# State updates of a chunked mLSTM layer as three products of rounded halves, with one buffer for the sample states

## What is computed

```python
num = (w_inter[..., None] * jnp.einsum('bthd,bhde->bhte', qb, C)
       + jnp.einsum('bhts,bshe->bhte', S, vb))
...
C_new = w_C[..., None, None] * C + jnp.einsum('bhs,bshd,bshe->bhde', w_s, kb, vb)
n_new = w_C[..., None] * n + jnp.einsum('bhs,bshd->bhd', w_s, kb)
```

## Time and profile before

| what | us |
|---|---|
| median of 3 runs (2037.6 to 2041.7) | 2039.84 |
| the profiled execution | 2038.48 |
| its span, first to last instruction | 2036.7 |
| busy in the span: PE / DVE / ACT / POOL | 2019.5 / 1426.9 / 922.5 / 876.6 |
| chain that ended last, by engine | PE 94%, SP queue 2%, DMA, DVE, ACT and issue 1% each |

### The profile page before, as it was taken

One profiled execution on the slowest core, in us unless ns is written; L12 is line 12 of the kernel. 1 busy time (PEld: TensorE's weight loads), 2 busy tenths in 40 slices (PEclk: granted clock), 3 DMA queues, 4 the chain that ended last, 5 costly groups with the idle time before them and its releaser, 6 DMA issues.

```text
span 2036.7 us, 34175 instructions
## 1 busy us (share of the span) xinstructions
PE 2019.5 (99%) x12259; PEld 1887.3 (93%) x12259; DVE 1426.9 (70%) x2214; ACT 922.5 (45%) x1886; POOL 876.6 (43%) x721
## 2 busy tenths in 40 slices
PE   9999999999999999999999999999999999999998
PEld 5999999999999999999999999998888888888886
DVE  7667676688777676798778766664445477777775
ACT  5544445545454445445454455442224343333332
POOL 2465556575655655684555555520000123222220
PEclk9999999999999999999999999999999999999999
DMA  6643555555444565555434566568645788888765
GB/s 223 149 124 114 143 142 140 146 133 127 124 129 128 136 160 145 125 139 133 122 115 125 141 162 132 132 204 208 166 119 174 207 253 269 247 239 239 235 180 120
DMA packets 551255, 328.24 MB, mean 161 GB/s; under 512 B 283440, under 2 KB 514736, under 8 KB 551088
## 3 DMA queue, kind: packets, MB, share of 16 engines
q1 hardware_dynamic: 512960, 307.45, 56.0%
q10 hardware_dynamic: 36976, 14.42, 2.9%
q0 software_dynamic: 1152, 4.19, 0.6%
HBM read 232.42 MB, written 93.57 MB: 160 GB/s over the span
## 4 chain that ended last, share of the span: by engine, by line
PE 94%; SPq 2%; DMA 1%; DVE 1%; ACT 1%; issue 1%; POOL 0%; DVEq 0%; POOLq 0%; ACTq 0%
PE bank L712 21%; PE bank L714 21%; PE bank L713 21%; PE bank L2297 3%; PE bank L2299 2%; PE bank L2298 2%; PE bank L2267 2%; PE bank L2252 2%; PE bank L1663 1%; PE bank L1665 1%; PE bank L1664 1%; PE bank L1649 1%; PE bank L1652 1%; PE bank L1650 1%; PE bank L1614 1%; PE bank L780 1%
## 5 line engine op out<-in xcount | busy, mean ns | idle before, releaser
L712 PE MATMUL bank<-xh,wh 128*128 128x352 f32 x2688 | 869.5, 323 | 2.0 <-ACT snap L882 1.6
L714 PE MATMUL bank<-xh,wl 128*128 128x352 f32 x2688 | 866.3, 322 | 0.0
L713 PE MATMUL bank<-xl,wh 128*128 128x352 f32 x2688 | 863.0, 321 | 0.0
L1097 DVE TENSOR_TENSOR wl<-raw,wh 128x512 fp32r<-128x512 f32 x384 | 421.6, 1100 | 209.1 <-ACT wh L860 207.9
L712 PEld LDWEIGHTS bank<-xh,wh 128*128 128x128 f32 x2688 | 504.4, 188 | 5.2 <-issue 2.0
L714 PEld LDWEIGHTS bank<-xh,wl 128*128 128x128 f32 x2688 | 506.9, 189 | 0.0
L713 PEld LDWEIGHTS bank<-xl,wh 128*128 128x128 f32 x2688 | 506.0, 188 | 0.3 <-issue 0.2
L882 ACT ACTIVATE snap<-bank 128x352 f32<-128x352 f32 x384 | 178.4, 465 | 375.7 <-PE bank L714 375.6
L860 ACT ACTIVATE wh<-raw 128x512 fp32r<-128x512 f32 x384 | 240.7, 628 | 157.2 <-PE bank L714 155.7
L1097 DVE TENSOR_TENSOR wl<-wt,wh 128x512 fp32r<-128x512 f32 x288 | 235.4, 822 | 103.6 <-ACT wh L860 103.2
L660 POOL TENSOR_TENSOR stage<-snap 128x352 f32<-128x352 f32 x96 | 96.4, 1004 | 460.5 <-ACT snap L882 459.2
(11 more groups left out here) (349 smaller groups left out, 2584.4 us busy)
## 6 DMA issues: line engine op xcount, KB each, us to landing
raw<-in_w_in SPq DMA_DIRECT2D x72, 1024.0 KB, 5.7
raw<-in_w_in SPq DMA_DIRECT2D x48, 512.0 KB, 5.4
scr_vob<-stage SPq DMA_DIRECT2D x192, 88.0 KB, 3.7
scr_qk<-stage SPq DMA_DIRECT2D x48, 352.0 KB, 5.9
raw<-scr_qk SPq DMA_DIRECT2D x16, 1024.0 KB, 8.5
area<-scr_vob SPq DMA_DIRECT2D x32, 512.0 KB, 8.0
scr_acc<-x_res SPq DMA_DIRECT2D x17, 512.0 KB, 6.1
m_acc<-scr_acc SPq DMA_DIRECT2D x17, 512.0 KB, 8.0
```

The lines of the kernel that those rows point to most:

```text
L712: pe.matmul(out, wh[:, b, k, :], xh[:, b, k, :], start=(first and k == 0), stop=False, skip_group_check=True)
L713: pe.matmul(out, wh[:, b, k, :], xl[:, b, k, :], start=False, stop=False, skip_group_check=True)
L714: m = pe.matmul(out, wl[:, b, k, :], xh[:, b, k, :], start=False, stop=(k == 3), skip_group_check=True)
L1097: dve.tensor_tensor(low, source(q, b), high.bitcast(F32), ALU.subtract).then_inc(S["w_low"], 1)
```

## The change

From tile 2 on, the keys and values of the state update are split in two: ScalarE copies the weighted keys and the values with ones to rounded ones (`high`: 128x1024 each), VectorE subtracts the rounded keys from the keys (`keys_low`, in place of the keys), GpSimd the rounded values from the values (`values_low`). The update is then three products, high x high, low x high (258 columns each) and high x low (256), instead of one fp32 product. The room comes from the second buffer of the sample states: there is now one, so a unit's states are loaded once the previous unit's have been stored, and the store is issued in the unit's own tile. Arrangement and addresses besides that:

```diff
         syhl = overlay(4 * D, "m_s_y", [P, 8, 2, TS], F32R)
+        kwl0 = overlay(8 * D, "m_kwl0", [P, H, HD], F32R)
         convw = sb(ctx, "convw", [P, 2, 4, D], F32R)
...
     UNIT_LOADS = 10
-    SQUARES_FROM = 2
+    SQUARES_FROM = SPLIT_FROM = 2
     qk = qk_tiles(raw)
...
     th = [th0, wide[:, 0:1024]]
     qs = wide[:, 1024:2048].rearrange("p (f t) -> p f t", f=8)
-    kw = [a.rearrange("p (h d) -> p h d", h=H) for a in (wide[:, 2048:3072], overlay(22560, "m_kw1", [P, D])[:, :])]
+    kw = [a.rearrange("p (h d) -> p h d", h=H) for a in (wide[:, 2048:3072], overlay(22656, "m_kw1", [P, D])[:, :])]
+    kwh, kwl = overlay(0, "m_kwh", [P, H, HD], F32R), (kwl0, overlay(22656, "m_kwl1", [P, H, HD], F32R))
+    v1l, v1h = overlay(4096, "m_v1l", [P, H, HD], F32R), overlay(26752, "m_v1h", [P, H, 288], F32R)
     kb = overlay(18464, "m_kb", [P, D])
     C = wide[:, 3072:5128].rearrange("p (h d e) -> p h d e", h=H, d=2)
-    sC = (wide[:, 5128:7184].rearrange("p (b d e) -> p b d e", b=4, d=2), overlay(0, "m_s_C", [P, 4, 2, HE]))
+    sC = wide[:, 5128:7184].rearrange("p (b d e) -> p b d e", b=4, d=2)
     sq, sz, sbr = (wide[:, at:at + 128].rearrange("p (r d x) -> p r d x", r=2, d=2) for at in (7184, 7312, 7440))
...
     def states_loaded(u):
-        return S[f"states_loaded{u % 2}"], 32 * (u // 2 + 1)
+        return S["states_loaded"], 32 * (u + 1)
 
     def load_states(dma, u):
-        (i, h), p = unit(u), u % 2
+        if u >= UNITS:
+            return
+        i, h = unit(u)
+        wait(dma, S["s_stored"], 32 * u)
         for d in range(2):
             at = slice(d * P, (d + 1) * P)
-            dma.dma_start(sC[p][:, :, d, 0:HD], st_C[0, 4 * i:4 * i + 4, h, at, :].rearrange("b p e -> p b e")).then_inc(states_loaded(u)[0], 16)
+            dma.dma_start(sC[:, :, d, 0:HD], st_C[0, 4 * i:4 * i + 4, h, at, :].rearrange("b p e -> p b e")).then_inc(states_loaded(u)[0], 16)
 
...
             return
-        wait(dma, S[f"s_stored{u % 2}"], 32 * (u // 2))
         wait(dma, S["s_y_turned"], u - 1)
...
         load_keys(dma, u)
         load_rest(dma, u)
-        load_states(dma, u)
 
...
         def store_unit(u):
-            (i, h), p = unit(u), u % 2
+            i, h = unit(u)
             sp.wait_ge(S["s_C_updated"], 4 * (u + 1))
             for d in range(2):
                 at = slice(d * P, (d + 1) * P)
                 sp.dma_start(C_sample[0, 4 * i:4 * i + 4, h, at, :].rearrange("b p e -> p b e"),
-                             sC[p][:, :, d, 0:HD]).then_inc(S[f"s_stored{p}"], 16)
+                             sC[:, :, d, 0:HD]).then_inc(S["s_stored"], 16)
 
...
             residual(t)
-            if back_of(t - 1) is not None:
-                store_unit(back_of(t - 1))
             if t:
                 values(t + 2)
+                if back_of(t - 1) is not None:
+                    load_states(sp, back_of(t - 1) + 1)
                 key_squares(t + 2)
                 out_gates(t + 2)
+            if back_of(t) is not None and t < NT - 1:
+                store_unit(back_of(t))
             gates(t + 1)
...
         sp.wait_ge(S["state_stored"], 48)
-        sp.wait_ge(S["s_stored0"], 32 * 4)
-        sp.wait_ge(S["s_stored1"], 32 * 4)
+        sp.wait_ge(S["s_stored"], 32 * UNITS)
 
...
         pool.wait_ge(S["set"], 3)
+        def values_low(t):
+
+            pool.wait_ge(S["v_high"], t - SPLIT_FROM + 1)
+            pool.tensor_tensor(v1l[:, :, :], v1[t % 2][:, :, 0:HD], v1h[:, :, 0:HD].bitcast(F32), ALU.subtract).then_inc(S["v_low"], 1)
+
         for t in range(NT):
+            if t >= SPLIT_FROM:
+                values_low(t)
             ahead(t + 1)
...
                 h, d = j // 2, j % 2
-                if d == 0:
-                    pe.wait_ge(S["kw_ready"], 4 * t + h + 1)
-                m = pe.matmul(out, kw[t % 2][:, h, d * P:(d + 1) * P], v1[t % 2][:, h, :], start=True, stop=True)
+                dk = slice(d * P, (d + 1) * P)
+                if t < SPLIT_FROM:
+                    if d == 0:
+                        pe.wait_ge(S["kw_ready"], 4 * t + h + 1)
+                    m = pe.matmul(out, kw[t % 2][:, h, dk], v1[t % 2][:, h, :], start=True, stop=True)
+                else:
+                    if j == 0:
+                        pe.wait_ge(S["kw_low"], t - SPLIT_FROM + 1)
+                        pe.wait_ge(S["v_low"], t - SPLIT_FROM + 1)
+                    both = bank[DC[j % 2]][:, 0:HE + 1]
+                    pe.matmul(both, kwh[:, h, dk], v1h[:, h, 0:HE + 1], start=True, stop=False)
+                    pe.matmul(both, kwl[t % 2][:, h, dk], v1h[:, h, 0:HE + 1], start=False, stop=False)
+                    m = pe.matmul(both[:, 0:HD], kwh[:, h, dk], v1l[:, h, :], start=False, stop=True)
             else:
...
                 for j in range(4):
-                    pe.matmul(bank[SPARE][32 * j:32 * j + DT, 0:HE], sqs[:, d, DT * j:DT * (j + 1)], sC[p][:, j, d, :],
+                    pe.matmul(bank[SPARE][32 * j:32 * j + DT, 0:HE], sqs[:, d, DT * j:DT * (j + 1)], sC[:, j, d, :],
                               start=(d == 0), stop=False, skip_group_check=True)
...
 
+        def high(t):
+
+            if not SPLIT_FROM <= t < NT:
+                return
+            act.wait_ge(S["dC_summed"], updates_before(t - 1) + 8)
+            act.wait_ge(S["kw_ready"], 4 * t + 4)
+            act.activation(kwh[:, :, :], kw[t % 2], ACT.Copy).then_inc(S["kw_high"], 1)
+            act.wait_ge(S["v_ready"], 2 * t + 2)
+            act.wait_ge(S["v_padded"], 1)
+            act.activation(v1h[:, :, 0:HE], v1[t % 2], ACT.Copy).then_inc(S["v_high"], 1)
+
         def squares(t):
...
                 unit_front(front_of(t))
+            high(t + 1)
             y_high(t)
...
 
+        def keys_low(t):
+
+            if not SPLIT_FROM <= t < NT:
+                return
+            dve.wait_ge(S["kw_high"], t - SPLIT_FROM + 1)
+            dve.tensor_tensor(kwl[t % 2][:, :, :], kw[t % 2], kwh[:, :, :].bitcast(F32), ALU.subtract).then_inc(S["kw_low"], 1)
+
         def turn_o(t):
...
             for b in range(4):
-                c = sC[p][:, b, :, 0:HD]
+                c = sC[:, b, :, 0:HD]
                 dve.scalar_tensor_tensor(c, c, swcb[:, h, 4 * i + b:4 * i + b + 1],
...
         def unit_weights(u):
             dve.wait_ge(*unit_loads(u))
-            dve.tensor_copy(sC[u % 2][:, :, :, HD], n_of(u)).then_inc(S["s_n_set"], 1)
+            dve.tensor_copy(sC[:, :, :, HD], n_of(u)).then_inc(S["s_n_set"], 1)
             dve.wait_ge(S["s_kw_ready"], u + 1)
...
                     last_add(1)
+                    dve.memset(v1h[:, :, HE:HE + 1].bitcast(F32), 0.0).then_inc(S["v_padded"], 1)
             second_half(t)
...
             y_low(t)
+            keys_low(t + 1)
         dve.wait_ge(S["s_y_high"], 1)
```

More of the change, by code:

```diff
@@ L137, in layer @@
                work[:, 2104:2112], mem_k, mem_v, mv_prompt, w_out, x_prompt, x_sample, st_n)
-        recur(nc, block, X, M, overlay, bank, w, ident, raw, last_y, work, wide, syhl, area, nT, mask, smask, columns, late_w, res, yh, yl,
+        recur(nc, block, X, M, overlay, bank, w, ident, raw, last_y, work, wide, syhl, kwl0, area, nT, mask, smask, columns, late_w, res, yh, yl,
               wmh, wml, g_final, st_C, C_prompt, n_prompt, C_sample, n_sample, y_prompt, y_sample)
@@ L1922, in back_of, with recur @@
     return t // 2 if t > 0 and t % 2 == 1 and t // 2 < UNITS else None
-def recur(nc, block, before, S, overlay, bank, w, ident, raw, last_y, work, wide, syhl, area, nT, mask, smask, columns, late_w, res, yh, yl,
+def recur(nc, block, before, S, overlay, bank, w, ident, raw, last_y, work, wide, syhl, kwl0, area, nT, mask, smask, columns, late_w, res, yh, yl,
           wmh, wml, g_final, st_C, C_prompt, n_prompt, C_sample, n_sample, y_prompt, y_sample):
@@ L2722, in update @@
                 (i, h), p = unit(back_of(t)), back_of(t) % 2
-                n = sC[p][:, :, :, HD]
+                n = sC[:, :, :, HD]
                 ch.step(dve.tensor_tensor(n, n, swcb[:, h, 4 * i:4 * i + 4].unsqueeze(2).broadcast_to([P, 4, 2]), ALU.mult))
```

## The result

| | before | after |
|---|---|---|
| median (4 runs each, same chip) | 2038.84 us (2037.6 to 2041.7) | **2069.12 us** (2068.22 to 2073.78) |
| ratio, 95% interval | | 1.0157 [1.0145, 1.0170] |
| profiled execution | 2038.48, span 2036.7 | 2069.74, span 2067.5 |

What follows compares the result with a forecast made beforehand. The prediction took TensorE to bound the kernel. Its terms, 28.2 + 0.5 - 7.3 - 1.0 = +20.4 us on the profiled 2038.48, gave 2058.9, or 2060 us on the median; range 2045 to 2074 (0.80).

Steps and rivals of the forecast that it cites:

- Products: State updates on TensorE: three products at 0.12 us each instead of 0.425 per fp32 update, saving 7.3 us in all.
- Rival F: State updates: a product costs 0.16 us, so updates are not shortened; +13.5 us on A, 2074 us; chance 0.08.
- Taking turns: Odd tiles: VectorE and GpSimd each wait for the other's whole instruction, making VectorE 4.9 us late in tile 9.
- B: Odd tiles: VectorE's three subtractions run in a row after values_low, or sharing is more even; +10.7 us, 2051; chance 0.20.
- C: Odd tiles: values_low collides with nothing; stall 1.1 us in seven tiles, 2039 us in all; chance 0.07.
- The waits: TensorE at updates 0 and 1 of odd tiles: 4.2 us in tiles 3 to 13, 2.95 in tile 15, sum 28.2.
- Rival D: Update 1: VectorE under 0.8 us late stays covered, nothing stalls, 8.3 us are won, 2031.5 us; chance 0.07.
- The clock: TensorE's granted clock was taken to stay at 1.00, as it had where TensorE idled 1.0 us; no cost.
- rival E: Clock at the 1.2 GHz level while waits last: 2.8 us more in each of seven tiles, +19.6, 2080 us; chance 0.06.
- A: The main forecast: turns, waits and savings as summed, 2060 us on the median; alone 2054 to 2067; chance 0.52.
- Even tiles: VectorE's update 0 moves to just when TensorE's update 2 wants it: 0.1 us a tile, 0.5 in sum.
- Single buffer: State loads and stores: loads arrive in time, and a shorter SP queue at the start removes TensorE's idling there, -1.0 us.

Runs made afterwards that it cites:

- copies first: The changed kernel with ScalarE's two copies issued ahead of the sample unit's front instead of behind it: 2049.27 us, ratio 1.0052.
- small copy early: The copies first kernel with VectorE's 128x8 copy into the states' last column moved ahead of turn_o, no groups moved: 2041.82 us, ratio 1.0014.
- products only: The changed kernel with the splitting of keys and values left out in tiles 3 to 15, the three products kept: 2030.52 us, ratio 0.9958.
- filled waits: The changed kernel with five unused 512-column products before update 0 and nine before update 1 in odd tiles: 2057.79 us, ratio 1.0096.
- split only: The changed kernel with one fp32 product of low keys and values in place of the three, all splitting kept: 2072.98 us, ratio 1.0171.

## Why the prediction was right, and where it was short

Forecast and measurement, term by term; the measured ones are start-to-start distances in the two traces.

| term | forecast | measured |
|---|---|---|
| TensorE's waits in odd tiles | +28.2 | +23.8 |
| half clock behind these waits | 0 | +13.5 |
| even tiles | +0.5 | about +2 |
| cheaper products | -7.3 | about -8 |
| single buffer | -1.0 | +0.3 |
| sum | +20.4 | +31.6 (span: +30.8) |

**Products.** Right. The starts are 1866.34, .46 and .58, as forecast. An update with its three output products repeats after 1.06 us, where the kernel before has 1.13. Rival F (0.16) falls.

**Taking turns.** Right, step by step. In tile 9's times plus 11.67 us the working of the forecast reads: values_low over at 1853.07, y_low's first half at 1853.63, the mask add at 1854.76, the second half at 1855.32, keys_low at 1857.00. The trace has 1852.82, 1853.36, 1854.49, 1855.04 and 1856.71, the same order 0.3 us earlier throughout, since GpSimd's subtraction took 2.18 us instead of 2.37 and ScalarE was 0.87 us late instead of 1.04. The Trainium skill, page "SBUF — State Buffer", section "Who interferes with whom", calls the shared pair a lock under which the other engine is blocked for the whole instruction; the six turns here agree with it (y_low's halves at 2257 and 1749 ns, keys_low at 1.75 us). Rivals B (VectorE keeps its turn) and C (no collision) fall with this order, and the run without GpSimd's subtraction shows the price: 30 us.

**The waits.** Right in place, a little too large. VectorE's numerator was read 4.35 us late where 4.9 were forecast, and the two waits of a tile add up to 1.20 + 2.63 = 3.83 us against the old distances (the 0.07 us that update 0 saves added, as in the forecast), in tiles 5 to 13; 4.2 were forecast. In tiles 3 and 15 update 0 doesn't wait and the sum is 2.5 and 2.2. 5 x 3.83 + 2.47 + 2.2 = 23.8. (The forecast's 2.95 for tile 15 doesn't follow its own rule, by which 3.9 us late gives a stall of 3.2; 2.2 came.) Rival D (VectorE's lateness stays covered) falls: the cover at update 1 was 0.84 us, the lateness 4.35.

**The clock** is the step that failed. The forecast kept the clock at 1.00 because the only idle stretch of the profile before, 1.0 us, had not moved it; this was rival E, with a chance of 0.06. It came **on top of** A, in six of the seven odd tiles. In tiles 7, 9, 11 and 13 updates 1, 2 and 3 with their groups take 5.74 us instead of 3.17: 2.57 more in each of these tiles. In tiles 5 and 15 it is 1.6, in tile 3 nothing, 13.5 in all. The page "TensorE: Matmul & The Clock Gate" of the Trainium skill, part 1, says that idleness brings the clock to half; the trace agrees (0.50). Its waits of 1.1 and 2.2 us, one behind the other with 1.6 us of matmuls between them, were enough in each of the five tiles that have both. Single waits did it at times: 2.1 us in tile 15, but not 2.2 us in tile 3 (1.3 us for the states stood ahead of it there), and not the 2.8 to 3.1 us for the states in three of the experiments. What tells these apart no run shows; a wait's length alone doesn't. Rival E's own size was nearly right: 2.8 us a tile were put down for it, 2.57 and 1.6 came. A with E summed to 2080; with the smaller waits and in six tiles it is the 2069 measured. That this lies inside the range of 2045 to 2074 is luck: A alone ended at 2067, and the range went to 2074 for rival F, whose 13.5 us happened to be as much as the clock's. Two of the forecast's own signs of being wrong came with it: a clock below 1.00, and a wait on the states' DMA.

**Even tiles.** The forecast was 0.1 us a tile. Update 1 follows update 0 after 2.05 us, where about 1.75 was due; this is about 0.3 in each, 2 in sum. Which of VectorE's two late operations causes it (the add of the bank, the first state update) wasn't taken apart.

**Single buffer.** Half right, and small. The 1.0 us for which TensorE idled ahead of scores(3) is gone, as forecast; a wait of 1.3 us for the states of unit 1 has come. The forecast looked for the load's cover in tile 9, where it holds; the one place in which it doesn't hold is unit 1, whose load stands behind the first tiles' transfers. The wait there was between nothing and 3.5 us in the traces (nothing in two, one of which issues this load earlier); with the buffer alone the median did not move.

The span grew by 10.4 us more than forecast: 13.5 of the clock, less 4.4 for the shorter waits, and 2.1 in the small terms; the table has 0.8 too much. It is good to a us or two: the changed kernel's trace was already 1.0 us later ahead of its first update in tile 1.

## What to carry to other kernels

A wait on a TensorE-bound path can have two prices: its length, and what TensorE then does at 1.2 GHz; here the second was more than half of the first, so filling waits with useless products was worth 11 us, and moving useful groups into them 16. Before an elementwise step goes to GpSimd, list what VectorE does with two SBUF operands (or as a plain copy) in its shadow: a 2.18 us instruction whose own engine was 56% idle cost 30 us, and the order in which its input was issued on a third engine decided 20 of them.

## What the runs showed of the hardware that was not expected

- Two waits of 1.1 and 2.2 us, neither long by itself, took the granted clock from 1.00 to 0.50, and it stayed there for 5.5 us of unbroken matmuls. With the same lateness and TensorE busy it stayed at 1.00. Where a tile had one wait, it fell in three of the six tiles with 2.1 to 2.2 us (copies first), and in none at 1.3 to 1.6 us (small copy early).
- A longer wait didn't always lower it: behind the wait for the states of unit 1 it stayed at 1.00 after 2.8, 3.0 and 3.1 us (products only, filled waits, no subtraction on GpSimd), and fell to 0.50 after 2.5 and 3.5 us (split only, single buffer alone).
- A tiny VectorE instruction pays in full, too: a copy of 128x8 from SBUF to SBUF took 1.76 us instead of 0.17, as it stood behind a GpSimd subtraction of 128x1024. That copies take part in the contention is also in the Trainium skill's page "SBUF — State Buffer", same section; this run agrees.
- GpSimd's subtraction of 128x1024 took 2.18 us, less than the line through its two smaller sizes gave (2.37).
